# Two last weight pieces of a projection in tile order from tile 1 of 4, and tile 1 of the turned result split ahead of the last tile's norm

## What is computed

```python
def first_block(...):
    for l in range(2):
        y = hybrid_mixer(x, ...)                 # latent attention and a convolution, then @ w_o
        x = layer_norm(ALPHA * x + y, ln1_g[l], ln1_b[l])
        y = memory_cross_attention(x, mem, ...)  # x @ w_q, attention over 256 rows, then @ w_o
        x = layer_norm(ALPHA * x + y, ln2_g[l], ln2_b[l])
        y = swiglu_ffn(x, ...)                   # (silu(g) * up) @ w_down, 2816 hidden columns
        x = layer_norm(ALPHA * x + y, ln3_g[l], ln3_b[l])
def second_block(x, ...):
    h = x + hybrid_mixer_2(rms_norm(x), ...)     # windowed attention and retention, then @ w_out
    h = h + hierarchical_moe(rms_norm(h), ...)   # 64 experts, 2 of them per token
    return rms_norm(h)
```

## Time and profile before

| | |
|---|---|
| median of 3 runs | 3571.17 us (3569.41 to 3573.1) |
| the profiled execution's own time | 3575.26 us |
| its span, first to last instruction | 3573.4 us |
| TensorE's mean granted clock | 0.954 of full speed |
| PE busy | 3258.4 us, 91% |
| DVE busy | 1321.7 us, 37% |
| ACT busy | 875.4 us, 24% |
| chain that ended last | PE 66%, DMA 17%, DVE 10%, ACT 3%, POOL 2% |

### The profile page before, as it was taken

One profiled execution on the slowest core, in us unless ns is written; L12 is line 12 of the kernel. 1 busy time (PEld: TensorE's weight loads), 2 busy tenths in 40 slices (PEclk: granted clock), 3 DMA queues, 4 the chain that ended last, 5 costly groups with the idle time before them and its releaser, 6 DMA issues.

```text
span 3573.4 us, 35777 instructions
## 1 busy us (share of the span) xinstructions
PE 3258.4 (91%) x15128; PEld 2248.8 (63%) x15128; DVE 1321.7 (37%) x2223; ACT 875.4 (24%) x1387; POOL 131.4 (4%) x122
## 2 busy tenths in 40 slices
PE   6998899999998899998999999899699999999994
PEld 5677677877667677876888867677343333433331
DVE  3675443335675443335333444533311111111112
ACT  2342322222342322222233431122111111111111
POOL 0000000001000000001100000000100000000001
PEclk9999999999999999998999999899799999999997
DMA  4122122223112122322211321023599999999996
GB/s 153 59 71 83 59 83 92 97 98 117 59 62 92 59 83 92 103 102 85 74 54 54 94 75 53 33 92 143 209 425 426 426 425 426 426 425 426 426 426 240
DMA packets 229493, 627.62 MB, mean 176 GB/s; under 512 B 14736, under 2 KB 136464, under 8 KB 179920
## 3 DMA queue, kind: packets, MB, share of 16 engines
q1 hardware_dynamic: 207312, 579.37, 41.8%
q10 hardware_dynamic: 19824, 37.77, 3.0%
q0 software_dynamic: 2192, 8.13, 0.8%
HBM read 600.32 MB, written 22.81 MB: 174 GB/s over the span
## 4 chain that ended last, share of the span: by engine, by line
PE 66%; DMA 17%; DVE 10%; ACT 3%; POOL 2%; issue 2%; ACTq 0%; DVEq 0%; POOLq 0%
PE bank L120 64%; DMA piece<-in_moe_w 4%; DMA piece_high<-in_moe_w 3%; DMA mT_slot<-in_moe_w 3%; DMA xT<-in_moe_w 3%; DVE gate_acc L138 2%; PE bank L123 2%; DVE x_tok L138 1%; POOL root L135 1%; DMA memT<-in_moe_w 1%; DMA norm_room<-in_moe_w 1%; DMA y_att_slot<-in_moe_w 1%; DVE stat L153 1%; DVE piece_rounded L135 1%; ACT piece_high_rounded L126 1%
## 5 line engine op out<-in xcount | busy, mean ns | idle before, releaser
L120 PE MATMUL bank<-xT_rounded,piece_high_rounded 128*128 128x512 f32 (+1 forms) x1408 | 554.7, 394 | 25.1 <-DVE xT_low_rounded L135 25.1
L135 DVE TENSOR_TENSOR piece_rounded<-piece,piece_high_rounded 128x2048 fp32r<-128x2048 f32 (+1 forms) x156 | 342.1, 2199 | 575.2 <-ACT piece_high_rounded L126 574.8
L120 PE MATMUL bank<-xT_rounded,piece_rounded 128*128 128x512 f32 (+1 forms) x1408 | 542.1, 385 | 0.0
L120 PE MATMUL bank<-xT_low_rounded,piece_high_rounded 128*128 128x512 f32 (+1 forms) x1408 | 538.2, 382 | 0.0
L135 DVE TENSOR_TENSOR gate_and_hidden<-gate_and_hidden,bank 64x512 f32<-64x512 f32 x64 | 69.2, 1081 | 837.0 <-ACT gate_and_hidden L126 837.0
L126 ACT ACTIVATE piece_high_rounded<-piece 128x2048 fp32r<-128x2048 f32 (+1 forms) x156 | 283.0, 1820 | 287.6 <-DMA piece<-in_ffn_w_down 119.1
L120 PEld LDWEIGHTS bank<-xT_rounded,piece_high_rounded 128*128 128x128 f32 x1408 | 270.2, 192 | 80.9 <-DVE xT_low_rounded L135 26.3
L120 PEld LDWEIGHTS bank<-xT_low_rounded,piece_high_rounded 128*128 128x128 f32 x1408 | 269.9, 192 | 56.0 <-issue 4.4
L120 PEld LDWEIGHTS bank<-xT_rounded,piece_rounded 128*128 128x128 f32 x1408 | 268.4, 191 | 56.5
L120 PE MATMUL bank<-piece,xeT 128*64 128x512 f32 x488 | 239.1, 644 | 18.7 <-DMA piece<-in_moe_w 7.3
L120 PE MATMUL bank<-piece_high,xeT 128*64 128x512 f32 x464 | 185.3, 633 | 14.4 <-DMA piece<-in_moe_w 9.5
(11 more groups left out here) (337 smaller groups left out, 5054.3 us busy)
## 6 DMA issues: line engine op xcount, KB each, us to landing
piece<-in_moe_w SPq DMA_DIRECT2D x90, 1024.0 KB, 16.5
piece_high<-in_moe_w SPq DMA_DIRECT2D x88, 1024.0 KB, 16.5
xT<-in_moe_w SPq DMA_DIRECT2D x59, 1024.0 KB, 16.7
mT_slot<-in_moe_w SPq DMA_DIRECT2D x58, 1024.0 KB, 17.3
piece<-in_ffn_w_in SPq DMA_DIRECT2D x40, 1024.0 KB, 5.0
memT<-in_moe_w SPq DMA_DIRECT2D x30, 1024.0 KB, 15.8
y_att_slot<-in_moe_w SPq DMA_DIRECT2D x30, 1024.0 KB, 16.5
norm_room<-in_moe_w SPq DMA_DIRECT2D x29, 1024.0 KB, 17.0
```

The source lines that it names most:

```text
L120: return self.engine.matmul(*a, **k) if self.engine is not None else Nothing()
L135: return self.engine.tensor_tensor(*a, **k) if self.engine is not None else Nothing()
```

## The change

The group of tiles 0 and 1 is taken apart: with the last two pieces, tile 0 now gets its unit of n0 and of n1, then tile 1 both, then 2, then 3. Tile 1 is turned on PE between tile 3's two units (`turned(1)`, called once n0 has been released), and its split on DVE is moved from behind tile 3's norm to ahead of tile 3's addition. At the merge `turned(1)` does nothing.

```diff
--- before.py
+++ after.py
@@ -737,12 +737,14 @@
                     behind_first()
         if turned:
             n0, n1 = self.pe_piece(e, label), self.pe_piece(e, label)
-            for tiles in ((0, 1), (2,), (3,)):
+            for tiles in ((0,), (1,), (2,), (3,)):
                 for k0, n in ((starts[-2], n0), (starts[-1], n1)):
                     for i in tiles:
                         self.out_tile_pe(e, key, kt, lhs, lhs_ready, 1, k0, n, i)
                     if tiles[-1] == NT - 1:
                         self.release(e, n)
+                        if k0 == starts[-2]:
+                            turned(1)
                 if tiles == (2,):
                     turned(0)
 
@@ -1338,8 +1340,7 @@
                             lambda k, i: (self.yT[k][:, i * P:(i + 1) * P], self.yT_low[k][:, i * P:(i + 1) * P]),
                             lambda k0: [("z_split" if k0 else "y_split", l, k) for k in range(CT)],
                             lambda i: self.rows_to_T_pe(e, f"xT_mix{l}", i, self.x_tok, f"mix{l}", "normed", i), z_back)
-        for i in (1, 2):
-            self.rows_to_T_pe(e, f"xT_mix{l}", i, self.x_tok, f"mix{l}", "normed", i)
+        self.rows_to_T_pe(e, f"xT_mix{l}", 2, self.x_tok, f"mix{l}", "normed", 2)
 
         for j in range(KD // 2):
             n = self.pe_piece(e, "cross query")
@@ -1397,8 +1398,7 @@
                             lambda k, i: (self.oT[:, k, i * P:(i + 1) * P], self.oT_low[:, k, i * P:(i + 1) * P]),
                             [("xo_split", l, h, v) for h in range(XH) for v in range(2)],
                             lambda i: self.rows_to_T_pe(e, f"xT_cross{l}", i, self.x_tok, f"cross{l}", "normed", i))
-        for i in (1, 2):
-            self.rows_to_T_pe(e, f"xT_cross{l}", i, self.x_tok, f"cross{l}", "normed", i)
+        self.rows_to_T_pe(e, f"xT_cross{l}", 2, self.x_tok, f"cross{l}", "normed", 2)
 
     def project_out_act(self, e, label, kt, begun=0):
         for _ in range(begun, 2 * len(range(0, kt, SLOT // BANK))):
@@ -1477,8 +1477,9 @@
             self.low_of(e, low, low, self.yT[CT + c4]).then_inc(*e.tick("z_split", l, c4))
         x_from = (lambda i: ("x_landed",)) if l == 0 else (lambda i: (f"ffn{l - 1}b", "normed", i))
         def turned(i):
-            if i >= 2:
-                self.rows_to_T_dve(e, f"xT_mix{l}", i - 2, self.xT, self.xT_low)
+            if i == 2:
+                for j in (0, 1):
+                    self.rows_to_T_dve(e, f"xT_mix{l}", j, self.xT, self.xT_low)
 
         self.project_out_dve(e, f"mix{l}", "mix out", KD, ALPHA, True, x_from, turned, begun=1)
         for i in range(2, NT):
@@ -1516,8 +1517,9 @@
                                     self.oT[:, 2 * h + v, :]).then_inc(*e.tick("xo_split", l, h, v))
 
         def turned(i):
-            if i >= 2:
-                self.rows_to_T_dve(e, f"xT_cross{l}", i - 2, self.xT, self.xT_low)
+            if i == 2:
+                for j in (0, 1):
+                    self.rows_to_T_dve(e, f"xT_cross{l}", j, self.xT, self.xT_low)
 
         self.project_out_dve(e, f"cross{l}", "cross out", KD, ALPHA, True, lambda i: (f"mix{l}", "normed", i), turned)
         for i in range(2, NT):
@@ -1562,7 +1564,7 @@
                                 lambda k, i: (self.hidT[:, k, i * P:(i + 1) * P], self.hidT_low[:, k, i * P:(i + 1) * P]),
                                 [("hid_split", l, c) for c in range(f0, f1)],
                                 (lambda i: self.ffn_turned_pe(e, l, i)) if part == "b" else None)
-        for i in range(1, NT):
+        for i in (2, 3):
             self.ffn_turned_pe(e, l, i)
 
     def ffn_turned_pe(self, e, l, i):
@@ -1645,8 +1647,9 @@
                 def turned(i):
                     if l + 1 == DEPTH and i:
                         self.rms_dve(e, i - 1, self.xn_tok[:, i - 1, :], self.mix_gain, "mix_norm", ("mix_gain_landed",))
-                    if i >= 2:
-                        split(i - 2)
+                    if i == 2:
+                        for j in (0, 1):
+                            split(j)
 
                 def split(i):
                     if l + 1 < DEPTH:
@@ -2207,6 +2210,8 @@
                 banks.give(("m_branch", branch, c), "m_half", branch, c)
             self.release(e, n)
         def turned(i):
+            if i:
+                return
             for n, slot in enumerate(self.early_slots):
                 self.add_slot(f"early{n}", slot, "pe", "m_branch", "retention", KD - 1)
             for j in (0, 1):
```

## The result

The changed kernel takes 3549.6 us (median of 4, 3547.7 to 3549.98), the kernel before 3572.1 in the same session. The ratio is 0.9937, 95% interval 0.992 to 0.9954. The forecast was 3551.8, in a range of 3548 to 3560. The same program timed in two more sessions took 3549.3 and 3549.9, against 3570.6 and 3569.2 for the kernel before: 21.3 and 19.4 us less.

The account below looks back on a forecast made before the run. PE, busy 91% of the span, was held at four stage ends by tile 1's split queued on DVE behind tile 3. Terms -20.2 + 1.2 + 0.05 - 0.4 = -19.4 from 3571.2 gave 3551.8 us, range 3548 to 3560.

Parts of the forecast that it names:

- The four places: Ends of mix 0, cross 0, mix 1, cross 1: PE's product starts earlier with tile 1's split moved; together 20.2 us won.
- The clock: At the four places: full granted clock assumed for the first product, about 2.9 us, despite remaining stops of about 1 and 1.6.
- The clock rival: At the four places the first product stays at half rate: 1.8 us lost at each, sum -12.2, 3559.0 us; chance 0.15.
- Ffn 0: First feed-forward: nobody waits early for tile 1's split, so tile 3's norm ends 1.20 us later; loss 1.2, bounds 0 to +1.5.
- Ffn 1: Second feed-forward: moved turn delays tile 3's sum 1.25 us, split out of the way returns 1.20; +0.05, fallen clock +2.8.
- Merge: At the merge tile 0 is summed a unit earlier, the 0.74 stop goes, a 0.3 wait comes; -0.4, bounds -0.7 to 0.
- the rival that it is lost in the experts' stage: Experts' stage: transfers bound by something that doesn't move, so the time stays 3571; chance 0.03.
- late high part: DVE waits for tile 1's high part: 2 us lost at each of four places, sum -11.4, 3559.8 us; chance 0.03.
- tile 3's norm as the bound all along: PE's next real need is tile 3: early start lost, 1.20 added at five places, +6.0, 3577.2 us; chance 0.04.

Follow-up runs that it names:

- the split's place alone: The changed kernel with tiles 0 and 1 summed together again, so only tile 1's turn and split are moved: 3552.3 us, ratio 0.9949.
- the order alone: The kernel before with only the tile order of the last two pieces changed, tile 1's turn and split left behind tile 3: 3570.4 us, ratio 1.0.
- the last version: The changed kernel, feed-forward places put back, tile 3's turn inside the second product, half of tile 0's split in the root's wait at mix and cross: 3542.7 us.

## Why the prediction was right

**The four places, -20.2.** Right as a mechanism and to 0.03 us a place. The start hung on tile 1's split (the split's place alone wins -20.2 at these four; the order alone wins nothing there). Behind it the bound was tile 3's norm, 1.20 us later, and two runs show it: 1.20 us more of DVE's work ahead of that norm cost 1.18 at cross 1, where the clock held, and a cut product in the stop of 1.5 us won 1.0 at each place.

**The clock.** I had no row for whether stops of about 1 and 1.6 us would keep it high. They did: 1.00 in the rows above, and at all four places in all three traces of the changed kernel. The only row for it was of other stops, in the cross attention, so this term was a bet that came out, not something worked out. The clock rival, and the Trainium skill's page behind it ("TensorE: Matmul & The Clock Gate", section "HAM oscillation — how this bites in real kernels"), did not decide here. I had stretched that section: the waits that it tells of are of some 3 to 5 us, and the two here were 1.1 to 1.4 and 1.5. But it was near: 1.2 us more in the second stop brought a fall of the clock in at three places of four. That fall cost 1.5 a place. The one that I had priced at 1.8, with the first product at half rate too, no run of the changed order shows.

**Ffn 0, +1.2.** 1.19. Putting it back won 1.20 in the trace; in the time it can't be seen.

**Ffn 1, +0.05.** -0.07 in two traces of the changed kernel and +0.17 in the third. Tile 3's addition stood 1.4 us later behind the weight split (23.58 against 22.19; forecast 1.25), and tile 1's split out of the way gave 1.20 of it back. The other traces with the old order there have +0.02 to +0.28, so this place can't tell +0.05 from nothing. The stop at the moved turn, 0.2 by my working, was 1.5 in two traces, where the clock had come back earlier, and 0.12 in the third; either way the turn started when the norm let it. The working for a fallen clock has a slip: twice 2.07 is 4.1, not 3.9, so its bound was +2.9, not +2.8.

**Merge, -0.4.** -0.41, with the wait for n1's split at 0.27 where 0.3 was worked out. I had left that wait out of the additions' times: tile 1's came 10.88 us behind the start of the weight split, not 10.24 (2480.5 less 2470.26). It still was early enough to take away the stop of 0.74.

**The sum.** The shift reached the end whole; the rival that it is lost in the experts' stage fell. Against the medians the forecast is 2.2 us short in time, or 22.5 won against 19.4, and in two further sessions 21.3 and 19.4 were won. The rest is inside the interval. The lower end of the forecast's own range is not what its terms give: with both feed-forward places at nothing and the merge at -0.7 the sum is -20.9, and the time 3550.3, not 3548. The measured 3549.6 lies below that, by no more than the runs scatter. The step that I did not have is that the kernel has several stops, of 0.5 to 5 us, behind which PE's restart takes 1.5 us more or less from one execution to the next. I compared one execution with one sum; the second trace of before, 6.0 us shorter than the first with the same program, shows how little one span says.

**The rivals with a late high part and with tile 3's norm as the bound all along** fell with the rows above; the second was true at ffn 0, as said.

## What to carry to other kernels

When one engine works a queue in order, look for the instruction whose data is long there and whose reader stands still; moving it ahead of a whole tile's work costs only its own length to that tile, and that price has to be paid again wherever nobody waits for the moved one. After the move ask at once what the next stop is and what work is queued behind it: cutting a product in two to fill a stop of 1.5 us won another 4 us in the places, and moving half of a split into DVE's wait for POOL's root 2 more. And where the differences are some microseconds in thousands, read them place by place in the trace: where the clock held, the time of a place repeated within 0.03 us between executions. Where it fell, at the ends of mix 0 and cross 0 in the kernel before, two traces differed by 1 us, and whole executions of that kernel differed by up to 7 (3566.7 to 3573.9 in one session).

## What the runs showed of the hardware

- The same instructions restart differently after the same stop: behind one of 5.0 us the window of 5.9 us shown above holds 14 and 18 matmuls in the two traces of the kernel before (granted clock 0.50 and 0.71), and 20 in one of the changed kernel (0.76). The same eight matmuls took 3.70 and 5.16 us in two traces of the changed kernel. Steps of 1.0 to 3.2 us a stretch made 6.0 us between two traces of one program.
- Some such steps go with the program: +1.2 to +1.8 us ahead of cross 1 and -1.6 ahead of ffn 1 in three traces of the changed kernel out of three, none in the two of before.
- Within one place a stop of 1.5 us left the granted clock at 1.00; one of 2.7 us was followed by 0.65 at mix 0, and the place grew by 1.5 us more than the stop at three places of four.
- One program had medians of 3549.8 and 3544.2 us in two sessions on two chips, with no overlap of their five runs each, while the kernel before had 3570.8 and 3569.2 and the last version 3542.7 twice.
